# Decoder layer with 32 experts: ScalarE's queue begins the first two gate-up pieces of most experts

## The reference, cut to what matters

```
gu = xb @ w_gu[e] + b_gu[e]            # 1024 x 2048 weights
gate = jnp.minimum(gu[:, :D_FF], 7.0)
up = jnp.clip(gu[:, D_FF:], -7.0, 7.0)
act = gate * jax.nn.sigmoid(gate * 1.702) * (up + 1.0)
y = act @ w_down[e] + b_down[e]        # 1024 x 1024 weights
y * gw[:, None], summed over a token's four experts
```

## Time and profile before

| | |
|---|---|
| median of 3 runs | 1020.58 us (1018.58 to 1020.58) |
| the profiled execution | 1020.94 us, span 1019.1 us |
| TensorE busy | 955.1 us (94%) |
| VectorE, ScalarE busy | 204.6 us (20%), 116.9 us (11%) |
| moved | 418.88 MB, mean 411 GB/s |
| mean granted clock of TensorE | 0.995 of full speed |

### The profile page before, as it was taken

How to read it: one execution, slowest core, us unless ns; L and a number is a source line. 1 busy time by engine, 2 the same in 40 slices (tenths; PEclk the granted TensorE clock), 3 DMA queues, 4 the chain that set the end, 5 groups by cost and what they waited for, 6 DMA issues and landing times.

```text
span 1019.1 us, 11373 instructions
## 1 busy us (share of the span) xinstructions
PE 955.1 (94%) x4541; PEld 375.6 (37%) x4541; DVE 204.6 (20%) x625; ACT 116.9 (11%) x250; POOL 16.3 (2%) x10
## 2 busy tenths in 40 slices
PE   7999999999999999999999999999999999999997
PEld 4555533333333333333233333333333333333342
DVE  2746211111111111211012111110112111101121
ACT  2431100010001000010001000010001000000011
POOL 0023000000000000000000000000000000000000
PEclk9999999999999999999999999999999999989999
DMA  9996799999999999999999999999999999999996
GB/s 367 382 404 237 288 428 428 426 429 426 427 430 428 427 430 428 428 430 428 428 429 427 430 429 427 429 429 427 430 427 429 408 426 426 428 428 427 429 420 240
DMA packets 33741, 418.88 MB, mean 411 GB/s; under 512 B 3888, under 2 KB 4272, under 8 KB 8400
## 3 DMA queue, kind: packets, MB, share of 16 engines
q1 hardware_dynamic: 33424, 418.39, 97.6%
q10 hardware_dynamic: 288, 0.07, 0.0%
HBM read 417.40 MB, written 1.05 MB: 411 GB/s over the span
## 4 chain that ended last, share of the span: by engine, by line
PE 54%; DMA 41%; DVE 3%; ACT 1%; issue 1%; SPq 0%; DVEq 0%; ACTq 0%
DMA ring<-w_gu_dram 40%; PE ps L1057 25%; PE ps L1135 14%; PE ps L1031 4%; PE ps L1016 4%; PE ps L920 3%; PE ps L858 2%; PE ps L1102 1%; DMA ring<-w_qkv_dram 1%; PE ps L1109 1%; ACT PR L503 1%; PE ps L1159 0%; PE ps L900 0%; DVE PR L669 0%; DVE passing L673 0%
## 5 line engine op out<-in xcount | busy, mean ns | idle before, releaser
L1057 PE MATMUL ps<-ring,PR 128*64 128x512 f32 x1008 | 230.3, 601 | 22.9 <-DMA ring<-w_gu_dram 22.3
L1057 PE MATMUL ps<-ring,passing 128*64 128x512 f32 x1008 | 228.2, 595 | 24.0 <-DMA ring<-w_gu_dram 24.0
L1135 PE MATMUL ps<-ring,PT 128*64 128x512 f32 x988 | 218.8, 595 | 0.5 <-DVE PT L826 0.5
L813 DVE TENSOR_SCALAR tT<-ps 128x256 f32<-128x256 f32 x64 | 27.2, 425 | 671.4 <-PE ps L1057 671.4
L1057 PEld LDWEIGHTS ps<-ring,PR 128*64 128x64 f32 x1008 | 71.3, 138 | 173.9 <-issue 126.8
L1057 PEld LDWEIGHTS ps<-ring,passing 128*64 128x64 f32 x1008 | 69.6, 137 | 173.8 <-issue 121.4
L1135 PEld LDWEIGHTS ps<-ring,PT 128*64 128x64 f32 x988 | 68.3, 137 | 129.5 <-issue 128.8
L552 ACT ACTIVATE tT<-tT 128x256 f32<-128x256 f32 x64 | 26.7, 417 | 493.6 <-DVE tT L813 493.6
L1031 PE MATMUL ps<-PT 64*128 64x512 f32 x256 | 71.7, 639 | 1.6 <-issue 1.6
L1016 PEld LDWEIGHTS ps<-qk,N 128*128 128x128 f32 x544 | 64.8, 196 | 21.6 <-issue 21.6
L1016 PE MATMUL ps<-qk,N 128*128 128x128 f32 x544 | 71.1, 285 | 0.8 <-DVE qk L784 0.8
(11 more groups left out here) (162 smaller groups left out, 357.2 us busy)
## 6 DMA issues: line engine op xcount, KB each, us to landing
ring<-w_gu_dram SPq DMA_DIRECT2D x123, 2048.0 KB, 31.2
ring<-w_down_dram SPq DMA_DIRECT2D x59, 2048.0 KB, 35.0
ring<-w_gu_dram SPq DMA_DIRECT2D x6, 1024.0 KB, 26.6
ring<-w_mix_dram SPq DMA_DIRECT2D x2, 2048.0 KB, 26.9
ring<-w_down_dram SPq DMA_DIRECT2D x4, 1024.0 KB, 30.1
ring<-w_down_dram SPq DMA_DIRECT2D x8, 512.0 KB, 29.9
ring<-w_qkv_dram SPq DMA_DIRECT2D x3, 768.0 KB, 11.7
ring<-w_u_dram SPq DMA_DIRECT2D x1, 2048.0 KB, 18.1
```

What stands on the lines that cost most here:

```text
L813: nc.vector.tensor_scalar(gb[:, b, :], gu[:, b, 0, :], LIMIT, None, ALU.min).then_inc(g_ready, 1)
L1057: last = mm(ps[64 * j:64 * j + 64, GU + b, :], lhs, halves[j][:, 512 * b:512 * b + 512], start=start, stop=stop)
L1135: last = mm(ps[64 * j:64 * j + 64, bank, :], at[:, k, 64 * (c - GU_PIECES):64 * (c - GU_PIECES) + 64], rows[:, 512 * j:512 * j + 512], sta ...
```

## The change

For experts 2 to 30, c0 and c1 are no longer issued by SyncE but by ScalarE. It issues the two for expert n + 2 right behind its instructions for expert n, the last of which is the copy in `down_out`, and without a wait of its own: the copy has waited for the count 6n + 6, which is what c1 needs (c0 needs 6n + 5). SyncE skips them, with their waits, and issues everything else as before, from its own queue. The first eight pieces, all of expert 31, and all c2 to c5 stay with SyncE. `landed` and TensorE's waits are the same.

```diff
             with sp.Fori(0, TURNS - 3) as r:
                 for s in range(TP):
-                    sp.wait_ge(pieces_used, r * TP + s + 1)
-                    load_piece(RING + s, r * TURN)
+                    if (RING + s) % PIECES >= 2:
+                        sp.wait_ge(pieces_used, r * TP + s + 1)
+                        load_piece(RING + s, r * TURN)
             for s in range(RING, 3 * TP - 2 * PIECES):
+                if s == TP + RING:
+                    sp.wait_ge(pieces_used, (TURNS - 3) * TP + s - RING + 1)
+                    sp.dma_start(bdn, b_down).then_inc(ld_bdn, 16)
+                if s % PIECES < 2:
+                    continue
                 sp.wait_ge(pieces_used, (TURNS - 3) * TP + s - RING + 1)
-                if s == TP + RING:
-                    sp.dma_start(bdn, b_down).then_inc(ld_bdn, 16)
...
             for n, (u, c) in enumerate(LAST_TWO):
                 s = 3 * TP - 2 * PIECES + n
+                if n < 2:
+                    continue
...
-            with act.Fori(0, TURNS - 1) as r:
-                turn_of_experts(r * TURN)
+            def load_gate_up(n, u, skip=0):
+
+                for c in range(2):
+                    slot = ((u + 2) * PIECES + c) % RING
+                    dst = ring[:, slot * PIECE:(slot + 1) * PIECE].rearrange("p (o n) -> p o n", o=1)
+                    part = slice(skip if c == 0 else 0, PIECE)
+                    act.dma_start(dst[:, :, part], w_gu_k[:, bass.ds((n + 2) * GU_PIECES + c, 1), part]).then_inc(landed[slot], 16)
+
+            with act.Fori(0, TURNS - 3) as r:
+                for u in range(TURN):
+                    expert(r * TURN + u, u)
+                    load_gate_up(r * TURN + u, u)
+            for n in range(NE - 3 * TURN, NE - TURN):
+                expert(n, n % TURN)
+                load_gate_up(n, n % TURN, 2 * FF if 0 <= n + 2 - (NE - 2 * TURN) < AHEAD else 0)
             for u in range(TURN):
                 expert(NE - TURN + u, u, (None, None, "last but one", "last")[u])
+                if u == 0:
+                    load_gate_up(NE - TURN, 0)
```

## The result

| | before | changed |
|---|---|---|
| median of 5 runs each | 1020.11 us (1018.22 to 1020.58) | 1024.52 us (1023.26 to 1024.93) |
| ratio of the runs | | 1.0047, 95% interval 1.0036 to 1.0059 |
| profiled execution, its span | 1020.94, 1019.1 us | 1024.74, 1022.9 us |
| mean granted clock | 0.995 | 0.985 |

The kernel became slower, by 4.4 us; two more series of the same changed kernel gave 1.0062 and 1.0059, that is 6 us. The prediction was 1027.6 us (+7.0), in a range of 1021 to 1033: the direction, the mechanism and the place were right, the size was too high, by 2.6 us against the first series and by 0.7 to 1.0 against the later ones.

The account below looks back on a forecast made before the run. Weight transfers at about 428 GB/s were taken to bound the loop, TensorE's own work the last 50 us. Terms 0 + 0 + 2.0 + 5.0 = +7.0 us on 1020.58 gave 1027.6 us, range 1021 to 1033.

Parts of the forecast that it names:

- Cover of ScalarE's issues: Behind ScalarE's result copy: two issues, 0.9 us, fit into 12.96 us of idle time and cost 0.
- The hole (2.0): Near 131.7 us: c0 of expert 2, issued one piece later, leaves transfers idle 1.7 to 2.3 us, taken as 2.0.
- Sharing (c5 9.8 us late): ScalarE's c0 and c1 share bandwidth with SyncE's waiting pieces, so the next expert's c5 lands 9.8 us late.
- One wait per expert, in c5, of 3.1 us, first in expert 5 near 259: TensorE's weight waits move from gate-up to down: one per expert, some 3.1 us, the first near 259 us.
- No wait after about 902: At the end of the loop TensorE waits for no weight after about 902 us.
- 27c5 lands at 901.8: Piece c5 of expert 27 lands at 901.8 us instead of 890.0, making TensorE 9.0 us late.
- The walk from there to the end: From expert 27's c5 to the end: TensorE 9.0 us late, old waits vanish in expert 30, 7.0 us remain.
- The clock (rival, 0.2): Behind expert 27's c5 wait the granted clock falls too, adding 2.7 us: +9.7, 1030.3 us; chance 0.2.
- The overtaking's share (5.0 of the 7.0): ScalarE's pieces passing SyncE's waiting ones make up 5.0 us of the 7.0 us lateness at the end.
- More bandwidth: Rival: two queues move more during the loop; 1.6% more rate gives 1014 us. Chance 0.12, plus 0.07 for just cancelling.
- less bandwidth: Rival: two queues move less or ScalarE's is starved; 1% lower is 8.4 us, 1036 and over; chance 0.09.
- one line: Rival: ScalarE's pieces overtake nothing, only the transfer gap near 131 us stays: +2.0, 1022.6 us; chance 0.1.

Follow-up runs that it names:

- the late c0, alone: Kernel before, with SyncE still issuing everything but c0 of each expert waiting for the count 6n + 6: +1.6 us, ratio 1.0016.
- the third execution: Profiled execution of the third series of the same changed kernel, against the kernel before: ratio 1.0059.
- the run with both undone: Changed kernel with SyncE again issuing c0 and c1 of expert 2 and of experts 22 to 30, ScalarE only 19 pairs: ratio 0.9998 to the kernel before.
- the run without a hole: Changed kernel with c0 and c1 of expert 2 issued by SyncE as before, all others by ScalarE: +3.6 us, ratio 1.0035 to the kernel before.

## Why the prediction was right, and where its sizes were off

**Cover of ScalarE's issues:** right. Two issues take 0.88 us, and the next work on that engine comes 13 us later, as before.

**The hole (2.0):** right. 1.9 us in the windows, +1.6 (0.8 to 2.5) by the run that has its cause, the late c0, alone. ScalarE issues beside its copy, the nearer of the two bounds.

**Sharing (c5 9.8 us late):** right, and now shown where it was only read off one small transfer: 9.82 us between two landings that lie 4.89 apart in one line. The Trainium skill (DMA: Bandwidth & Descriptors, Queues, rings and completion order) says that each DMA engine takes turns between the queues that have work for it, a packet at a time. The trace agrees as far as it goes: it shows half and half, not the single packets.

**One wait per expert, in c5, of 3.1 us, first in expert 5 near 259:** right but for details. The wait there ends at 260.88 after 2.90 us, in an execution 2.36 us ahead; expert 4 had a small one before, of 0.74. **No wait after about 902:** wrong, 29c5 is waited for (2.24 us, at 957.65).

**27c5 lands at 901.8:** 898.92 in a run that was 2.36 us ahead, so 901.3. **29c5 at 960.4:** 957.65, so 960.0.

**The walk from there to the end** is the step that failed in part. I let TensorE be 9.0 us late all along and gave 2.0 back in expert 30, where the old waits vanish, and nothing behind it ("the rest has no wait and moves as one"). Measured from expert 0, expert 30 begins at 858.7 where before it was 849.3: 9.4 late. From the start of expert 30 to the end of the span it then takes 60.1 us against 63.3: 3.2 came back, not 2.0. The terms: the old waits and what restarting behind them costs, 2.2 (expert 30 takes 19.3 us to the first gate-up matmul of expert 31, before 21.5); a wait for a piece in expert 31, 0.2; and 0.9 in front of the last matmuls, where before TensorE stood still for 1.65 us and now for 0.78:

```profile
1012.71 1.99 PE L1031 MATMUL ps<-PT 64*128 64x512 f32 x8 [1.65 <-issue]
...
1016.49 1.99 PE L1052 MATMUL ps<-PT 64*128 64x512 f32 x8 [0.78 <-ACT PT L573]
```

The first row is of before, the second of the changed kernel. The unnamed part of this wait (1.00 and 0.14 us) differs the same way in all eleven profiles: it is 0.14 in the five in which ScalarE issues the pair of expert 30, and 0.74 to 2.02 in the other six. So the kernel before had about 1 us of idle time at its very end for a late TensorE to use up. I hadn't read the rows behind 968 us for idle time, since the chain there named TensorE. So +7.0 should have been 9.4 − 3.2 = +6.2, and that is also what two of the three series give. The first series' 4.4 (by its interval 3.7 to 6.0) lies below; the clock's chance, in its five runs and in those of before beside it, is large enough for that, but it wasn't shown to be the cause.

**The clock (rival, 0.2):** it happened, though not where it was priced, and that 9.4 lies so near to 9.0 is in part luck. I had carried along the fall behind L1159, which is chance and was missing in the changed execution (3.70 and 13.10 us in place of 4.41 and 15.72), so TensorE came to 29c5 early enough to wait 2.24 us for it, and then paid another fall: 5.35 us for 16 matmuls in place of 3.65, 1.7 us. Without that fall expert 30 would have begun 7.7 us late and the change would have cost 4.5 us, an estimate from these rows. So two slips of mine, a lateness at 29c5 that wasn't there and a fall left out of the sum, nearly cancel. I had priced a fall behind 27c5 at 2.7; the third execution has it there. In the middle of the run the falls come behind every second or third wait and cost nothing, as supposed (the run with both undone has them too): the expert after one simply waits 1.2 to 1.5 in place of 2.9.

**The overtaking's share (5.0 of the 7.0):** too high, and the idle time behind 968 us that the walk left out is part of it. Alone it cost 3.6 us (2.2 to 4.9).

**More bandwidth, less bandwidth, one line:** out. 428 and 429 GB/s from 300 to 500 and from 500 to 700 us, where before it was 428, and the overtaking seen.

## What to carry to other kernels

Where transfers set the pace and every piece is needed in the order in which it is issued, one queue keeps that order, as it did here; moving some of the prefetches to a second queue let them take half the bandwidth from the pieces that were needed first. The bytes don't change, so nothing adds up from round to round: this lateness is had once and is given back in the consumer's spare time (3.1 us per expert here), and what counts is whether the end comes before it has been given back. A stretch in which no transfer runs is another matter: where transfers set the pace, it stays lost (+1.6 us with the late c0 alone). So look at the first and the last round of such a change, not at the number of rounds, and if a second queue is wanted for another reason, keep the last pieces and the first one in the old queue, which here brought the cost to nothing (0.9998).

## What the runs showed of the hardware that was not expected

The granted clock fell or did not in executions of the same kernel, at the same instruction: 0.60 or 1.00 at 100 us, 0.50 or 1.00 at 900 us in two executions of the kernel before. The spans of these two differ by 1.8 us, of which 1.5 are the start of expert 0. So a difference of 2 us can't be read from the spans of one profile each.

Waits of 2.9 us for a weight were followed by 16 matmuls at the full clock (3.65 us) as well as by matmuls at a lower clock (16 in 5.0 to 5.4 us, twice 6.6), the latter in 45 of 65 cases over the six profiles with such waits in front of c5. No wait of 1.2 to 1.5 us was followed by a lower clock in any of the eleven profiles; of two waits of 1.9 us one was (5.35 us, in the run without a hole), one wasn't (898.92). Rows for both kinds stand above (260.88 and 378.33).

A transfer that found all engines idle lost about 1.8 us from its issue, on SyncE's queue; the hole of 1.9 us in front of ScalarE's first one is of the same size.
